# TensorE's expert code as loops over pairs of experts, weight buffers with a period of two experts, and the last output weights in 1 MB pieces

## The chip, the core and the metric

The kernel runs on one core of one Trainium2 chip. Its time is the device time in microseconds (us) of one execution. The engines are TensorE (PE; PEld is its weight load), VectorE (DVE), ScalarE (ACT), GpSimd (POOL) and SyncE (SP). SP issues nearly all transfers; they run on the core's 16 DMA engines.

## The reference: what is computed

One layer on 256 tokens of 1024 float32 values: a norm and an input projection, a state-space branch and an attention branch that are gated and merged, an output projection, cross-attention to a memory of 256 tokens, and then a mixture of 32 experts, which is the part that the change touches:

```
logits = xf @ w_router + b_router ; the best 4 experts of each token, gates = softmax of their logits
for every expert e, with its tokens xb:
    hgl = xb @ w1[e] + b1[e]                        # 1024 -> 2048 (w1: 8.39 MB for one expert)
    glu = min(hgl[:, :1024], 7) ; lin = clip(hgl[:, 1024:], -7, 7)
    act = glu * sigmoid(1.702 * glu) * (lin + 1)
    y   = act @ w2[e] + b2[e]                       # 1024 -> 1024 (w2: 4.19 MB)
out[token] += gate * y ; then a last norm
```

Every weight of the 32 experts is read once from device memory: 32 x 12.58 MB = 402.7 MB.

## The kernel before

**Ahead of the experts** (until about 456 us) come the projections and attentions. Their tiles lie in one arena in SBUF of 25 pages of 1 MB (`PAGE` is 2048 float32 for each of 128 partitions). As pages come free, SP loads the first expert weights into them: 11 halves of 2 MB, each in two pieces of 1 MB (`piece`, L379).

**An expert on TensorE** is `item(i, parts)` (L1014 to L1024). An expert has 64 slots of tokens. In order: `weights_in` (64 matmuls at L965 against w1, in four halves of 2 MB), `scattered` (8 at L933: adds the result of the expert before to the tokens), `gather` (8 at L918: the tokens of the next expert), then transposes (L984 gates, L990 activations, L925 gathered tokens) and two bias matmuls (L941), and `weights_out` (32 at L1010 against w2, in two halves of 2 MB). ACT and DVE do the work between: clips and products (DVE L1780 to L1786), sigmoid (ACT L1340), copies out of PSUM (ACT L1324, L1344, L1348, and L1352 for the result `ys`). TensorE's program is written out: `expert(i)` is called for i = 0 to 29, with the matmuls of the output bias (L1066) between 15 and 16. ACT and DVE run their side of the experts in hardware loops.

**The last two experts** (`last_two`, L1026) are interleaved: input part of 30, its middle, input part of 31, output part of 30, activations of 31, scatter and gates, output part of 31. All of it goes through bank 3 of PSUM.

**The weight buffers.** The stream of weights is cut into chunks `n` of 4 MB, three for an expert: two of w1 and one of w2. `e_at(n)` gives the order, the order of use: (30, w1), (31, w1), (30, w2), (31, w2) at the end. For the first 22 halves, 11 buffers of 2 MB rotate. After that, five buffers of 4 MB rotate (`2 * ((n + 4) % 5) + h`), so chunk n goes where chunk n-5 was. From chunk 21 (expert 7) on, a chunk is one transfer of 4 MB (`whole`, L357); the last chunk of all goes in four pieces of 1 MB with semaphores of their own (L452).

**What orders the transfers.** SP runs one program: for each chunk in the order of the stream it waits until the chunk that lay in the buffer has been used (`e_free`: counters that TensorE raises at the end of each part), and then issues the next transfer. A wait of SP holds back all transfers behind it. All of them go into one queue (q1).

Of the kernel before, what the change touches and what calls it, by code (L numbers as in the profile page):

```python
# [17 lines left out]
D = 1024  # L18
# [14 lines left out]
CHUNKS = 3  # L33
BY_HALF = 21
LAST = CHUNKS * NE - 1
# [10 lines left out]
def layer_program(nc, x, mem, norm_mix_g, w_in, conv_w, conv_b, dt_bias, a_log, d_skip, ssd_norm_g,  # L46
# [52 lines left out]
    with ExitStack() as ctx:  # L99
# [84 lines left out]
        W_AT = (0, 2, 4, 6, 8, 10, 14, 16, 18, 20, 23)  # L184
        prow3 = late[0:2, 1536:2048]
# [114 lines left out]
        last_loaded = [sem(f"last_loaded{k}") for k in range(4)]  # L300
# [13 lines left out]
        def e_at(n):  # L314

            last = CHUNKS * (NE - 2)
            if n < last:
                return n // CHUNKS, n % CHUNKS
            return ((NE - 2, 0), (NE - 2, 1), (NE - 1, 0), (NE - 1, 1), (NE - 2, 2), (NE - 1, 2))[n - last]

        def e_source(n, h):

            i, s = e_at(n)
            if s < 2:
                return w_ein[0, i, 512 * s:512 * (s + 1), :].rearrange("(p h c) n -> p h (c n)", h=2, c=2)[:, h, :]
            return w_eout[0, i].rearrange("(p h c) n -> p h (c n)", h=2, c=4)[:, h, :]

        def e_slot(n, h):

            m = 2 * n + h  # L330
            return m % 11 if m < 22 else 2 * ((n + 4) % 5) + h

        def e_half(n, h):

            return page(W_AT[e_slot(n, h)], 2 * PAGE)

        def e_free(n, h):

            i, s = e_at(n)
            if s == 0:  # L340
                return e_used, 4 * i + h + 1
            if h:
                return (h_psum, y_psum)[s - 1], i + 1
            return e_used, 4 * i + 2 + s

        def by_half(n):
            return n < BY_HALF or n == LAST

        filled, loads = [0] * 11, {}
        for n_ in range(CHUNKS * NE):  # L350
            for h_ in range(2):
                b_ = e_slot(n_, h_) - (0 if by_half(n_) else h_)
                if h_ == 0 or by_half(n_):
                    filled[b_] += 32 if 2 * n_ + h_ < 11 else 16
                loads[n_, h_] = (e_loaded[b_], filled[b_])

        def whole(engine, expert, s, quad):  # L357

            to = page(W_AT[2 * quad], 4 * PAGE)
# [4 lines left out]
            engine.dma_start(to, source).then_inc(e_loaded[2 * quad], 16)  # L364
# [5 lines left out]
        def _(sp_):  # L370
# [8 lines left out]
            def piece(m, k):  # L379

                n, h, cols = m // 2, m % 2, slice(PAGE * k, PAGE * (k + 1))
                sp_.dma_start(e_half(n, h)[:, cols], e_source(n, h)[:, cols]).then_inc(e_loaded[e_slot(n, h)], 16)
# [21 lines left out]
            ahead = [(0, 0), (0, 1), (1, 0), (1, 1), (2, 0), (2, 1), (10, 0), (10, 1)]  # L404
            for u in range(unit("out", 3), unit("cv", 1)):
                load(u)
                if ahead:
                    if ahead[0] == (10, 0):
# [4 lines left out]
            piece(4, 0)  # L413
            load(unit("cv", 2))
            piece(4, 1)
# [4 lines left out]
            piece(3, 0)  # L420
            load(unit("co", 3))
            piece(3, 1)
            for h in range(2):
                piece(8, h)
            sp_.wait_ge(w_lo_ready, 2 * NU)
            for h in range(2):
                piece(6, h)
            sp_.wait_ge(w_done, 2 * NU)
            for m in (5, 7):
                for h in range(2):  # L430
                    piece(m, h)
            sp_.wait_ge(ms_psum, 2)
            for h in range(2):
                piece(9, h)
            sp_.dma_start(gfin, norm_final_g.partition_broadcast(P)).then_inc(ld_g, 16)

            owner = {e_slot(m // 2, m % 2): m for m in range(11)}
            for n in range(CHUNKS, CHUNKS * NE):
                for h in range(2):
                    m = 2 * n + h  # L440
                    if m < 11:
                        continue
                    b = e_slot(n, h)
                    was, owner[b] = owner[b], m
                    if by_half(n) or h:
                        sp_.wait_ge(*e_free(was // 2, was % 2))
                    if n < BY_HALF:
                        sp_.dma_start(e_half(n, h), e_source(n, h)).then_inc(e_loaded[b], 16)
                    elif n == LAST:
                        for k in range(2):  # L450
                            cols = slice(PAGE * k, PAGE * (k + 1))
                            sp_.dma_start(e_half(n, h)[:, cols], e_source(n, h)[:, cols]).then_inc(last_loaded[2 * h + k], 16)  # L452
                    elif h:
                        whole(sp_, *e_at(n), b // 2)
                if n == 5 * CHUNKS:
                    sp_.wait_ge(item_psum, 1)
                    sp_.dma_start(b2[0:NE, :], b_eout[0]).then_inc(ld_b2, 16)
# [4 lines left out]
            with sp_.If(n_items > NE):  # L462
                with sp_.Fori(NE, n_items) as i:
                    e = sp_.value_load(meta[0:1, bass.ds(i, 1)], min_val=0, max_val=NE - 1)
                    sp_.wait_ge(y_psum, i)
                    for s in range(CHUNKS):
                        whole(sp_, e, s, s)
# [80 lines left out]
        def _(pe):  # L548
# [450 lines left out]
            def weights_out(i, parts):  # L999
                pe.wait_ge(at_ready, i + 1)  # L1000
                for h in range(2):
                    w, loaded = parts[4 + h]
                    if loaded:
                        pe.wait_ge(*loaded)
                    for c in range(4):
                        if type(i) is int and i == NE - 1 and c % 2 == 0:
                            pe.wait_ge(last_loaded[2 * h + c // 2], 16)
                        for half in range(2):
                            at = D * c + 512 * half
                            last = mm(ps[64 * half:64 * (half + 1), 3, :], at_cols[:, c, h, :], w[:, at:at + 512],  # L1010
                                      start=(h + c == 0), stop=(h + c == 4))
                    last.then_inc((e_used, y_psum)[h], 1)

# [31 lines left out]
            place = {e_at(n): n for n in range(CHUNKS * NE)}  # L1045

            def parts_of(i):

                out = []
                for s in range(CHUNKS):  # L1050
                    n = place[i, s]
                    for h in range(2):
# [15 lines left out]
            for i in range(NE // 2, NE - 2):  # L1068
                expert(i)
            last_two(NE - 2)  # L1070
            with pe.If(n_items > NE):
                gather(NE + 1)
                gathered_transposes(NE + 1)
                next_bias(NE - 1)
                with pe.Fori(NE, n_items) as i:
                    item(i, [(page(W_AT[2 * s + h], 2 * PAGE), None if h else (e_loaded[2 * s], 16 * i + (filled[2 * s] - 16 * (NE - 1))))
                             for s in range(CHUNKS) for h in range(2)])
# [5 lines left out]
        def _(act):  # L1083
# [262 lines left out]
            def acts(i):  # L1346
                act.wait_ge(at_psum, i + 1)
                A(actT, ps[:, 0, :], ACT.Copy).then_inc(at_ready, 1)  # L1348

            def result(i):  # L1350
                act.wait_ge(y_psum, i + 1)
                A(ys, ps[:, 3, :], ACT.Copy).then_inc(y_ready, 1)  # L1352
# [480 lines left out]
```

## Time and profile before

| | |
|---|---|
| three runs | 1371.81, 1371.67, 1368.5 us; median 1371.67 |
| the profiled execution | 1372.18 us; span in the trace 1370.4 us, mean TensorE clock 0.984 |
| PE busy | 1313.5 us (96% of the span) |
| DVE, ACT, POOL busy | 425.8, 363.0, 34.0 us |
| DMA | 471.86 MB, 344 GB/s over the span |

"Busy" is the union of an engine's instructions. A matmul at L965 shows 592 ns, but they overlap: 64 of them take 13.9 us. Clock 1.00 is 2.4 GHz and 0.5 is 1.2 GHz. The span starts at the first instruction; every time below is in us from there.

### The profile page before, as it was taken

The numbers are of one execution on the slowest core, as the hardware profiler recorded it, in microseconds if no ns is written. First come the engines' busy times: TensorE is split into PE (matmuls) and PEld (weight loads), VectorE is DVE, ScalarE is ACT, GpSimd is POOL, SyncE is SP. The second block draws the span as 40 slices with busy tenths as digits, with TensorE's granted clock in tenths as the row PEclk, the third lists the DMA queues.
The fourth block names the chain that finished last, engine by engine and source line by source line (L and its number), as shares of the span: only waits on it lengthen the run. The fifth ranks groups of instructions, "written<-read, shape, count | busy, mean of one in ns | idle before, by whom it ended". The sixth has DMA issues, their size and how long they took to land.

```text
span 1370.4 us, 17367 instructions
## 1 busy us (share of the span) xinstructions
PE 1313.5 (96%) x7436; PEld 733.1 (53%) x7436; DVE 425.8 (31%) x808; ACT 363.0 (26%) x559; POOL 34.0 (2%) x57
## 2 busy tenths in 40 slices
PE   6999999999999999999999999999899999899997
PEld 6999999999999433333333333333333333333332
DVE  6775657576653311211121112111112111112111
ACT  4854446645443211111111111111111111111102
POOL 2001200001001000000000000000000000000000
PEclk8999999999999999999999999999999999999999
DMA  7545453478856999999999999999999999999994
GB/s 222 157 140 152 141 153 101 130 209 304 302 185 253 407 405 427 418 428 435 428 434 433 429 431 432 432 428 431 430 436 430 429 428 434 435 430 428 430 428 188
DMA packets 87180, 471.86 MB, mean 344 GB/s; under 512 B 7194, under 2 KB 68770, under 8 KB 70212
## 3 DMA queue, kind: packets, MB, share of 16 engines
q1 hardware_dynamic: 86880, 470.71, 85.2%
q8 instruction: 60, 0.98, 0.3%
q10 hardware_dynamic: 228, 0.07, 0.0%
q14 instruction: 12, 0.10, 0.0%
HBM read 469.72 MB, written 1.05 MB: 344 GB/s over the span
## 4 chain that ended last, share of the span: by engine, by line
PE 72%; DMA 25%; ACT 1%; DVE 1%; issue 0%; ACTq 0%; DVEq 0%
DMA arena<-in_w_expert_in 22%; PE ps L965 19%; PE ps L1010 12%; PE ps L617 8%; PE ps L618 7%; PE ps L619 7%; PE ps L933 3%; PE ps L918 3%; DMA arena<-in_w_expert_out 3%; PE ps L608 1%; PE ps L610 1%; PE ps L609 1%; PE ps L925 1%; PE ps L941 1%; PE ps L990 1%; PE ps L984 1%
## 5 line engine op out<-in xcount | busy, mean ns | idle before, releaser
L965 PE MATMUL ps<-arena 128*64 128x512 f32 x2048 | 460.6, 605 | 31.8 <-DMA arena<-in_w_expert_in 31.2
L965 PEld LDWEIGHTS ps<-arena 128*64 128x64 f32 x2048 | 148.3, 139 | 337.2 <-issue 289.0
L1780 DVE TENSOR_SCALAR arena<-ps 128x512 f32<-128x512 f32 x32 | 22.1, 691 | 670.3 <-PE ps L965 670.3
L1010 PE MATMUL ps<-arena 128*64 128x512 f32 x1024 | 226.8, 595 | 3.1 <-DMA arena<-in_w_expert_out 2.6
L617 PE MATMUL ps<-A_hi,w_hi 128*128 128x256 f32 x576 | 168.2, 292 | 5.9 <-DVE A_lo L1404 4.6
L618 PE MATMUL ps<-A_lo,w_hi 128*128 128x256 f32 x576 | 165.1, 287 | 0.0
L619 PE MATMUL ps<-A_hi,w_lo 128*128 128x256 f32 x576 | 165.0, 286 | 0.0
L1437 DVE TENSOR_TENSOR w_lo<-w_raw,w_hi 128x1024 fp32r<-128x1024 f32 x120 | 142.7, 1230 | 60.8 <-ACT w_hi L1116 60.5
L1010 PEld LDWEIGHTS ps<-arena 128*64 128x64 f32 x1024 | 71.1, 137 | 138.9 <-issue 138.2
L1340 ACT ACTIVATE arena<-arena 128x512 f32<-128x512 f32 x32 | 20.1, 629 | 446.4 <-DVE arena L1780 446.4
L1116 ACT ACTIVATE w_hi<-w_raw 128x1024 fp32r<-128x1024 f32 x120 | 120.1, 1048 | 25.7 <-DMA w_raw<-in_w_out 6.7
L617 PEld LDWEIGHTS ps<-A_hi,w_hi 128*128 128x128 f32 x576 | 112.7, 196 | 8.3 <-issue 7.0
L618 PEld LDWEIGHTS ps<-A_lo,w_hi 128*128 128x128 f32 x576 | 112.9, 196 | 0.1
L619 PEld LDWEIGHTS ps<-A_hi,w_lo 128*128 128x128 f32 x576 | 112.7, 196 | 0.0
L1352 ACT ACTIVATE arena<-ps 128x512 f32<-128x512 f32 x32 | 19.1, 597 | 243.9 <-PE ps L1010 243.9
L933 PE MATMUL ps<-arena 64*128 64x512 f32 x264 | 65.6, 615 | 0.7 <-ACT arena L1352 0.7
L918 PE MATMUL ps<-arena,wrt 128*64 128x512 f32 x256 | 62.0, 605 | 0.0
L933 PEld LDWEIGHTS ps<-arena 64*128 64x128 f32 x264 | 22.7, 186 | 42.5 <-issue 40.7
L1727 DVE TENSOR_TENSOR arena<-ps,prm 128x512 f32<-128x512 f32 x32 | 22.1, 691 | 73.8 <-PE ps L925 73.8
L1324 ACT ACTIVATE arena<-ps 128x512 f32<-128x512 f32 x32 | 19.1, 597 | 77.5 <-PE ps L918 77.5
L1340 ACT ACT_TABLE_LOAD x30 | 38.5, 1283 | 1.0 <-issue 0.5
L918 PEld LDWEIGHTS ps<-arena,wrt 128*64 128x64 f32 x256 | 15.6, 136 | 42.1 <-issue 42.1
(300 smaller groups left out, 1337.5 us busy)
## 6 DMA issues: line engine op xcount, KB each, us to landing
arena<-in_w_expert_in SPq DMA_DIRECT2D x50, 4096.0 KB, 38.3
arena<-in_w_expert_out SPq DMA_DIRECT2D x24, 4096.0 KB, 39.8
arena<-in_w_expert_in SPq DMA_DIRECT2D x20, 2048.0 KB, 15.2
w_raw<-in_w_in SPq DMA_DIRECT2D x32, 1024.0 KB, 5.5
arena<-in_w_expert_out SPq DMA_DIRECT2D x11, 2048.0 KB, 15.8
arena<-in_w_expert_in SPq DMA_DIRECT2D x16, 1024.0 KB, 9.8
arena<-in_w_expert_out SPq DMA_DIRECT2D x10, 1024.0 KB, 10.8
w_raw<-in_w_cross_kv SPq DMA_DIRECT2D x8, 1024.0 KB, 8.0
```

The source lines that it names most:

```text
L617: mm(o, w_hi[:, s, k, :], a_hi[:, k, :], start=(k == 0), stop=False)
L618: mm(o, w_hi[:, s, k, :], a_lo[:, k, :], start=False, stop=False)
L619: last = mm(o, w_lo[:, s, k, :], a_hi[:, k, :], start=False, stop=(k == KT - 1))
L918: last = mm(ps[64 * half:64 * (half + 1), 2, :], sel[:, 64 * tb:64 * (tb + 1)], xtok[:, tb, 512 * half:512 * (half + 1)], start=(tb == 0), ...
L933: last = mm(ps[:, 4 + 2 * tb + half, :], sgT[rows, tb * P:(tb + 1) * P], ys[rows, :], start=False, stop=bool(each), skip_group_check=True)
L965: last = mm(ps[64 * half:64 * (half + 1), b, :], xg_cols[:, 2 * h + c, s, :], columns[:, :, half, :], start=False, stop=(s + h + c == 3), ...
L1010: last = mm(ps[64 * half:64 * (half + 1), 3, :], at_cols[:, c, h, :], w[:, at:at + 512], start=(h + c == 0), stop=(h + c == 4))
L1116: A(w_hi[:, p % 4, :, :], raw_w[u % 2][:, :, j * P:(j + 1) * P], ACT.Copy).then_inc(w_hi_ready, 1)
L1340: A(sig, glu, ACT.Sigmoid, scale=ALPHA).then_inc(sig_ready, 1)
L1437: V_.tensor_tensor(w_lo[:, p % 4, :, :], raw_w[u % 2][:, :, j * P:(j + 1) * P], w_hi[:, p % 4, :, :].bitcast(f32), ALU.subtract).then_inc( ...
L1727: V_.tensor_tensor(xgT.rearrange("p (m a j) -> p m a j", m=4, a=2), ps[:, 2, :].rearrange("p (m a j) -> p m a j", m=4, a=2), prm[:, 136:14 ...
L1780: V_.tensor_scalar(glu, ps[:, 0, :], LIMIT, None, ALU.min).then_inc(glu_ready, 1)
```

## The change

Four things change together.

1. TensorE's program for experts 6 to 29 is two hardware loops over pairs of experts (`pairs(3, 5)` and `pairs(5, 15)`), two experts written out in the body. Semaphore targets are computed from the loop's register. Experts 0 to 5 are written out as before, and the output-bias matmuls lie between 9 and 10.
2. Buffers: w1 of an even expert lies in slots 0 to 3, of an odd one in 4 to 7, so w1 of expert i goes where w1 of i-2 was. w2 of experts 0 to 5 rotates over three halves (slots 8, 9, 10), and from expert 6 on it always lies in slots 8 and 9, one buffer of 4 MB. w2 of expert 31 goes to slots 0 and 1, where w1 of 30 was. SP issues transfers in the order in which the buffers come free: at expert i, first w1 of i+2, then w2 of i+1.
3. Whole transfers of 4 MB are used for experts 10 to 29 (before: 7 to 31 but for the last chunk).
4. w2 of experts 30 and 31 comes in eight pieces of 1 MB, each with its semaphore, and TensorE takes each by itself. The output part of 31 goes to bank 2 of PSUM and its activations to `xgT`, so its first piece stands ahead of the scatter of expert 30.

```diff
-CHUNKS = 3
-BY_HALF = 21
-LAST = CHUNKS * NE - 1
+BY_HALF = 10
+BY_THREE = 6
+LAST_TWO = NE - 2
...
-        last_loaded = [sem(f"last_loaded{k}") for k in range(4)]
+        last_loaded = [[sem(f"last_loaded{b}_{k}") for k in range(4)] for b in range(2)]
...
+        def e_slot(i, j):
+
+            if j < 4:
+                return 4 * (i % 2) + j
+            if i == NE - 1:
+                return j - 4
+            return 8 + ((2 * i + j - 4) % 3 if i < BY_THREE else j - 4)
...
+        def e_free(i, j):
+
+            if j in (3, 5):
+                return (h_psum if j == 3 else y_psum), i + 1
+            return e_used, 4 * i + min(j, 3) + 1
+
+        def whole(i, j):
+            return BY_HALF <= i < LAST_TWO
+
+        def in_pieces(i, j):
+            return i >= LAST_TWO and j >= 4
+
+        order = [(i_, j_) for i_ in range(LAST_TWO) for j_ in range(6)]
+        for js in (range(4), range(4, 6)):
+            order += [(i_, j_) for i_ in (LAST_TWO, NE - 1) for j_ in js]
+        follower, filled, loads, owner = {}, [0] * len(W_AT), {}, {}
+        for at in order:
+            b_ = e_slot(*at)
+            if b_ in owner:
+                follower[owner[b_]] = at
...
+            for was in order:
+                if was not in follower:
+                    continue
+                i, j = follower[was]
+                if j % 2 or not whole(i, j):
+                    sp_.wait_ge(*e_free(*was))
+                if in_pieces(i, j):
+                    for k in range(2):
+                        cols = slice(PAGE * k, PAGE * (k + 1))
+                        sp_.dma_start(e_half(i, j)[:, cols],
+                                      e_source(i, j)[:, cols]).then_inc(last_loaded[i - LAST_TWO][2 * (j - 4) + k], 16)
+                elif not whole(i, j):
+                    sp_.dma_start(e_half(i, j), e_source(i, j)).then_inc(e_loaded[e_slot(i, j)], 16)
+                elif j % 2:
+                    load_whole(sp_, i, j // 2, e_slot(i, j - 1))
...
+            def out_pass(cols, bank, w, h, c):
+
+                for half in range(2):
+                    at = D * c + 512 * half
+                    last = mm(ps[64 * half:64 * (half + 1), bank, :], cols[:, c, h, :], w[:, at:at + 512],
+                              start=(h + c == 0), stop=(h + c == 4))
+                return last
...
             def last_two(i):
 
-                first, second = parts_of(i), parts_of(i + 1)
-                weights_in(i, first)
+                def out_piece(b, cols, bank, k):
+
+                    pe.wait_ge(last_loaded[b][k], 16)
+                    for c in (2 * (k % 2), 2 * (k % 2) + 1):
+                        last = out_pass(cols, bank, e_half(i + b, 4 + k // 2), k // 2, c)
+                    return last
+
+                weights_in(i, parts_of(i))
                 scattered(i)
                 gather(i + 2)
                 gates(i)
                 acts(i)
                 gathered_transposes(i + 2)
                 next_bias(i)
-                weights_in(i + 1, second)
+                weights_in(i + 1, parts_of(i + 1))
                 pe.wait_ge(sgt_ready, i + 2)
-                weights_out(i, first)
+                pe.wait_ge(at_ready, i + 1)
+                for k in range(2):
+                    out_piece(0, at_cols, 3, k)
                 acts(i + 1)
+                out_piece(0, at_cols, 3, 2)
+                out_piece(0, at_cols, 3, 3).then_inc(y_psum, 1)
+                pe.wait_ge(at_ready, i + 2)
+                out_piece(1, xg_cols, 2, 0)
                 scattered(i + 1)
                 gates(i + 1)
+                for k in range(1, 4):
+                    last = out_piece(1, xg_cols, 2, k)
+                last.then_inc(y_psum, 1)
                 pe.wait_ge(sgt_ready, i + 3)
-                weights_out(i + 1, second)
...
+            def pair_parts(pair, first, i):
 
                 out = []
-                for s in range(CHUNKS):
-                    n = place[i, s]
-                    for h in range(2):
-                        own = n != LAST and (h == 0 or by_half(n))
-                        out.append((e_half(n, h), loads[n, h] if own else None))
+                for j in range(6):
+                    loaded = loads.get((i, j))
+                    if loaded:
+                        step = 32 if j >= 4 else 16
+                        loaded = loaded[0], step * pair + (loaded[1] - step * first)
+                    out.append((e_half(i, j), loaded))
                 return out
 
-            def expert(i):
+            def pairs(first, end):
+
+                with pe.Fori(first, end) as pair:
+                    for n in range(2):
+                        item(2 * pair + n, pair_parts(pair, first, 2 * first + n))
+
+            for i in range(BY_THREE):
                 item(i, parts_of(i))
-
-            for i in range(NE // 2):
-                expert(i)
+            pairs(BY_THREE // 2, BY_HALF // 2)
...
-            for i in range(NE // 2, NE - 2):
-                expert(i)
-            last_two(NE - 2)
+            pairs(BY_HALF // 2, LAST_TWO // 2)
+            last_two(LAST_TWO)
...
             sigmoid(NE - 1)
+            acts(NE - 1, xgT)
             result(NE - 2)
-            acts(NE - 1)
             gates(NE - 1)
-            result(NE - 1)
+            result(NE - 1, 2)
```

## Rows read from the trace of the kernel before

**Rows 1.** Windows of about one expert: busy us, clock, DMA share, GB/s.
```profile
core 0: us, PE busy (x) PEld busy (x) DVE busy (x) ACT busy (x) POOL busy (x), PEclk, DMA share, GB/s
460.00:489.20 29.20, 29.20 (x146) 11.18 (x142) 5.33 (x14) 6.29 (x12) 0.00 (x0) 1.00 0.94 373
489.20:518.40 29.20, 29.20 (x138) 10.43 (x136) 4.40 (x10) 3.94 (x6) 0.00 (x0) 1.00 1.01 430
576.80:606.00 29.20, 29.20 (x138) 10.25 (x134) 4.40 (x10) 3.94 (x6) 0.00 (x0) 1.00 1.01 430
1190.00:1219.20 29.20, 26.66 (x126) 9.67 (x124) 4.39 (x10) 3.95 (x6) 0.00 (x0) 1.00 1.00 430
```

**Rows 2.** TensorE in order of time (start, us, line): output of 16, expert 17.
```profile
920.56 7.09 PE L1010 MATMUL ps<-arena 128*64 128x512 f32 x32
927.48 13.90 PE L965 MATMUL ps<-arena 128*64 128x512 f32 x64
941.32 1.99 PE L933 MATMUL ps<-arena 64*128 64x512 f32 x8
947.13 7.09 PE L1010 MATMUL ps<-arena 128*64 128x512 f32 x32
```

**Rows 3.** The same view, stalls and clock at experts 15 and 19.
```profile
874.04 8.78 PE L965 MATMUL ps<-arena 128*64 128x512 f32 x32 [2.55 <-DMA arena<-in_w_expert_in]
991.83 7.09 PE L965 MATMUL ps<-arena 128*64 128x512 f32 x32 [2.46 <-DMA arena<-in_w_expert_in]
```

**Rows 4.** The same view, the tail: experts 29, 30 and 31.
```profile
1284.75 8.64 PE L965 MATMUL ps<-arena 128*64 128x512 f32 x32 [2.36 <-DMA arena<-in_w_expert_in]
1299.14 7.09 PE L1010 MATMUL ps<-arena 128*64 128x512 f32 x32
1306.06 7.04 PE L965 MATMUL ps<-arena 128*64 128x512 f32 x32
1313.90 7.09 PE L965 MATMUL ps<-arena 128*64 128x512 f32 x32 [0.81 <-DMA arena<-in_w_expert_in]
1320.92 1.99 PE L933 MATMUL ps<-arena 64*128 64x512 f32 x8
1327.01 13.95 PE L965 MATMUL ps<-arena 128*64 128x512 f32 x64 [0.20 <-DVE arena L1727]
1343.56 7.09 PE L1010 MATMUL ps<-arena 128*64 128x512 f32 x32 [2.60 <-DMA arena<-in_w_expert_out]
1350.58 0.75 PE L990 MATMUL ps<-ident,arena 128*128 128x128 f32 x4
1351.33 1.99 PE L933 MATMUL ps<-arena 64*128 64x512 f32 x8
1353.25 0.44 PE L984 MATMUL ps<-ident,arena 128*128 128x128 f32 x2
1354.16 7.09 PE L1010 MATMUL ps<-arena 128*64 128x512 f32 x32 [0.47 <-ACT arena L1344]
```

**Rows 5.** VectorE in order of time, activations of expert 31.
```profile
1341.01 0.69 DVE L1780 TENSOR_SCALAR arena<-ps 128x512 f32<-128x512 f32 x1 [13.22 <-PE ps L965]
1343.06 0.69 DVE L1786 TENSOR_TENSOR arena<-arena 128x512 f32<-128x512 f32 x1
```

**Rows 6.** Issues of SP in order of time.
```profile
1262.73 31.03 SPq L364 DMA_DIRECT2D arena<-in_w_expert_in  x4
1306.27 0.33 SPq L364 DMA_DIRECT2D arena<-in_w_expert_out  x1
1309.70 4.24 SPq L452 DMA_DIRECT2D arena<-in_w_expert_out  x4
```

**Rows 7.** The four pieces of the last chunk (L452), from issue to landing.
```profile
DMA to landing us min/median/max: 36.2/38.0/39.7
```

**Rows 8.** The page: busy time and instructions; the queue of instruction pages.
```profile
PE 1313.5 (96%) x7436; PEld 733.1 (53%) x7436; DVE 425.8 (31%) x808; ACT 363.0 (26%) x559; POOL 34.0 (2%) x57
q8 instruction: 60, 0.98, 0.3%
```

**Rows 9.** One window from expert 15's stall to expert 29's, columns as in rows 1.
```profile
874.04:1284.75 410.71, 388.65 (x1745) 136.61 (x1745) 61.55 (x140) 55.27 (x84) 0.00 (x0) 0.97 1.00 431
```

**Rows 10.** First loads: issues of SP; transfers at L448; the page's row of gfin.
```profile
444.24 4.20 SPq L382 DMA_DIRECT2D arena<-in_w_expert_in  x4
448.48 0.44 SPq L435 DMA_DIRECT2D gfin<-in_norm_final_g  x1
460.49 0.33 SPq L448 DMA_DIRECT2D arena<-in_w_expert_out  x1
...
482.68 0.33 SPq L448 DMA_DIRECT2D arena<-in_w_expert_in  x1
...
DMA to landing us min/median/max: 7.2/15.8/20.6
...
gfin<-in_norm_final_g SPq DMA_DIRECT2D x1, 512.0 KB, 13.5
```

**Rows 11.** TensorE in order of time, first output part and the next.
```profile
478.99 7.09 PE L1010 MATMUL ps<-arena 128*64 128x512 f32 x32
505.55 7.09 PE L1010 MATMUL ps<-arena 128*64 128x512 f32 x32
```

More of the change, by code:

```diff
@@ L184, in layer_program @@
         W_AT = (0, 2, 4, 6, 8, 10, 14, 16, 18, 20, 23)
+        EXTRA_AT = (0, 2, 8)
         prow3 = late[0:2, 1536:2048]
@@ L328, in e_slot @@
[L328 to L359, printed above, removed]
+        def e_slot(i, j):
[4 more added lines that the diff above has]
+            return 8 + ((2 * i + j - 4) % 3 if i < BY_THREE else j - 4)
@@ new lines, in e_half, with e_source @@
+        def e_half(i, j):
+            return page(W_AT[e_slot(i, j)], 2 * PAGE)
+        def e_source(i, j):
+            if j < 4:
+                rows = slice(512 * (j // 2), 512 * (j // 2 + 1))
+                return w_ein[0, i, rows, :].rearrange("(p h c) n -> p h (c n)", h=2, c=2)[:, j % 2, :]
+            return w_eout[0, i].rearrange("(p h c) n -> p h (c n)", h=2, c=4)[:, j - 4, :]
+        def e_free(i, j):
+            if j in (3, 5):
+                return (h_psum if j == 3 else y_psum), i + 1
+            return e_used, 4 * i + min(j, 3) + 1
@@ new lines, in whole @@
+        def whole(i, j):
[10 more added lines that the diff above has]
+                follower[owner[b_]] = at
+            if not in_pieces(*at) and not (whole(*at) and at[1] % 2):
+                filled[b_] += 16 if b_ in owner else 32
+                loads[at] = (e_loaded[b_], filled[b_])
+            owner[b_] = at
@@ L360, in whole, with load_whole @@
+        def load_whole(engine, expert, s, slot):
             if s < 2:
@@ L363, in whole @@
                 source = w_eout[0, expert].rearrange("(p c) n -> p (c n)", c=8)
-            engine.dma_start(to, source).then_inc(e_loaded[2 * quad], 16)
+            engine.dma_start(page(W_AT[slot], 4 * PAGE), source).then_inc(e_loaded[slot], 16)
         block = ctx.enter_context(nc.Block())
@@ L403, in _ @@
             sp_.wait_ge(b1_ready, 2)
-            ahead = [(0, 0), (0, 1), (1, 0), (1, 1), (2, 0), (2, 1), (10, 0), (10, 1)]
+            ahead = [(i, j, k) for i, j in ((0, 0), (0, 1), (0, 2), (1, 4)) for k in range(2)]
             for u in range(unit("out", 3), unit("cv", 1)):
@@ L407, in _ @@
                 if ahead:
-                    if ahead[0] == (10, 0):
+                    if ahead[0] == (1, 4, 0):
                         sp_.wait_ge(a_lo_ready, SPLIT["u2"] + 4)
@@ L412, in _ @@
             sp_.wait_ge(w_done, 2 * unit("cq", 3) + 2)
-            piece(4, 0)
+            piece(1, 0, 0)
             load(unit("cv", 2))
-            piece(4, 1)
+            piece(1, 0, 1)
             for u in range(unit("cv", 3), unit("co", 2)):
@@ L419, in _ @@
             load(unit("co", 2))
-            piece(3, 0)
+            piece(0, 3, 0)
             load(unit("co", 3))
-            piece(3, 1)
-            for h in range(2):
-                piece(8, h)
+            piece(0, 3, 1)
+            for k in range(2):
+                piece(0, 4, k)
             sp_.wait_ge(w_lo_ready, 2 * NU)
-            for h in range(2):
-                piece(6, h)
+            for k in range(2):
+                piece(1, 2, k)
             sp_.wait_ge(w_done, 2 * NU)
-            for m in (5, 7):
-                for h in range(2):
-                    piece(m, h)
+            for j in (1, 3):
+                for k in range(2):
+                    piece(1, j, k)
@@ L432, in _ @@
             sp_.wait_ge(ms_psum, 2)
-            for h in range(2):
-                piece(9, h)
+            for k in range(2):
+                piece(0, 5, k)
             sp_.dma_start(gfin, norm_final_g.partition_broadcast(P)).then_inc(ld_g, 16)
[L437 to L455, printed above, removed]
@@ new lines, in _ @@
+            for was in order:
[5 more added lines that the diff above has]
+                if in_pieces(i, j):
+                    for k in range(2):
+                        cols = slice(PAGE * k, PAGE * (k + 1))
+                        sp_.dma_start(e_half(i, j)[:, cols],
[4 more added lines that the diff above has]
+                    load_whole(sp_, i, j // 2, e_slot(i, j - 1))
+                if was == (4, 0):
@@ L465, in _ @@
                     sp_.wait_ge(y_psum, i)
-                    for s in range(CHUNKS):
-                        whole(sp_, e, s, s)
+                    for s in range(3):
+                        load_whole(sp_, e, s, EXTRA_AT[s])
             for tb in range(TB):
@@ L1005, in weights_out @@
                     for c in range(4):
[L1006 to L1011, printed above, removed]
-                    last.then_inc((e_used, y_psum)[h], 1)
+                        last = out_pass(at_cols, 3, w, h, c)
+                    last.then_inc((e_used, y_psum)[h], 1)
+            def out_pass(cols, bank, w, h, c):
[4 more added lines that the diff above has]
+                return last
             def item(i, parts):
@@ L1075, in _ @@
                 with pe.Fori(NE, n_items) as i:
-                    item(i, [(page(W_AT[2 * s + h], 2 * PAGE), None if h else (e_loaded[2 * s], 16 * i + (filled[2 * s] - 16 * (NE - 1))))
-                             for s in range(CHUNKS) for h in range(2)])
+                    item(i, [(page(W_AT[EXTRA_AT[s]] + 2 * h, 2 * PAGE),
+                              None if h else (e_loaded[EXTRA_AT[s]], 16 * i + (filled[EXTRA_AT[s]] - 16 * (NE - 1))))
+                             for s in range(3) for h in range(2)])
             pe.wait_ge(y_ready, n_items + 1)
@@ L1344, in gates, with acts, result @@
                 A(sgT, ps[:, 3, 0:S], ACT.Copy).then_inc(sgt_ready, 1)
-            def acts(i):
+            def acts(i, to=actT):
                 act.wait_ge(at_psum, i + 1)
-                A(actT, ps[:, 0, :], ACT.Copy).then_inc(at_ready, 1)
-            def result(i):
+                A(to, ps[:, 0, :], ACT.Copy).then_inc(at_ready, 1)
+            def result(i, bank=3):
                 act.wait_ge(y_psum, i + 1)
-                A(ys, ps[:, 3, :], ACT.Copy).then_inc(y_ready, 1)
+                A(ys, ps[:, bank, :], ACT.Copy).then_inc(y_ready, 1)
             def item(i):
```

21 lines of the change are left out of this document (5 added, 16 removed).

## The prediction

> **What bounds the kernel now.** I read the windows of one expert's length first. In the expert part the DMA engines move 430 GB/s at a busy share of 1.00 from the second window on, while TensorE's busy time falls from 29.20 of 29.20 us to 26.66 [rows 1]. So from some point the weights set the pace. Then TensorE in order of time. Without a stall one expert takes 947.13 - 920.56 = 26.57 us [rows 2]. With stalls, 14 experts (second w1 chunk of 15 to that of 29, 874.04 to 1284.75) take 410.71 us, 29.34 each [rows 3, 4], so a chunk of 4 MB takes 9.78 us. TensorE is 2.77 us an expert faster than its weights, and every expert waits once, for the second chunk of w1.
>
> The tail decides what the change is worth, so I read it instruction by instruction [rows 4]. The second w1 chunk of expert 30 is there at 1313.90. Four chunks follow it in the stream: 1313.9 + 4 x 9.78 = 1353.0 for the end of all loads. The last pieces say the same: issued from 1309.70 on, the last about 1313.6 [rows 6], landing within 39.7 us [rows 7], 1353.3. TensorE's last expert matmul ends at 1354.16 + 7.09 = 1361.25. So the tail behind the last byte is 8 us: TensorE reaches the output part of 30 at about 1341 (1327.01 + 13.95), waits until 1343.56 for its chunk as one whole, and has then 7.02 (output of 30), 0.75, 1.92, about 0.9 and 7.09 us of work in a row. After 1361.25 the same 9 us of scatter, norm and stores follow in both kernels.
>
> Three things are to be priced: when the loads end, what TensorE still has to do behind the load that holds it, and what the loops cost.
>
> **The order of the loads: this is the largest term.** Before, chunks arrive in the order in which they are used. After, SP issues w1 of i+2 when w1 of i has been read, and w2 of i+1 only when w2 of i has been read, which is behind it. Both go into one queue, and the last five issues, some 38 us from landing with four chunks ahead of them [rows 6, 7], say that this queue is served in order. So the stream at the end is w1(30), w2(29), w1(31), w2(30), w2(31), where it was w2(29), w1(30), w1(31), w2(30), w2(31). The chunk in front of the last four is now w2 of expert 29. It lands when w1 of 30 did, T = 1313.9, and only then can TensorE start the output part of 29. It has all of 30 and 31 still before it, on weights that are by then in place:
> - output of 29: 1306.06 - 1299.14 = 6.92 [rows 4]
> - input of 30: 941.32 - 927.48 = 13.84 [rows 2]
> - middle of 30: 1327.01 - 1320.92 = 6.09 [rows 4]
> - input of 31: 13.84, which makes 1354.59
> - output of 30, 7.02 (1350.58 - 1343.56), transposes 0.75, output of 31, 7.02, scatter 1.92 (1353.25 - 1351.33), gates 0.44 [rows 4]: 17.15
>
> This ends at 1371.74, against 1361.25: **+10.5 us**. Work in the tail has no load to wait for any more: the last byte is there at about 1353, before the input of 31 is done. Hence the pieces of 1 MB and their semaphores gain nothing by arriving early. What part 4 of the change does save is the 0.5 us wait of the last output part for ACT (0.47 in rows 4), and it is already in the sum. Its activations hide too: the chain on DVE takes 2.74 us from the end of the input (1341.01 to 1343.06 + 0.69, [rows 5]), and the two first pieces, 3.5 us, lie over it.
>
> Does TensorE wait long enough to arrive at T at all? Unstalled it would be at the output of 29 at 478.99 + 29 x 26.57 + 4 (bias) = 1253.5 [rows 2, 11], 60 us before T. Yes.
>
> **Do the DMA engines stay full with one buffer for w2?** When w2 of i has landed (t), the engines have w1 of i+2 ahead of them, 19.6 us. w2 of i+1 is issued at t + 6.9, 12.7 us before its turn. w1 of i+3 is issued from t + 6.9 + 13.8 on, its turn is at t + 29.3. So they stay full, and the stall only moves, from the second chunk of w1 to w2. Cost 0. If this cover went, each microsecond of a gap in every expert would cost 24 us.
>
> **First loads.** The same pages are filled in the same order; what changes is which weights lie in them. The second half of w2 of expert 0 becomes the last (issued by 448.4; the transfer behind it lands within 13.5 us, at 462, [rows 10]) and is needed at 478.99 + 3.5 [rows 11]. The second half of w2 of expert 1 is issued at 482.68 instead of 460.5, lands 7.2 to 20.6 us later, by 503.6 [rows 10], and is needed at 509.0 (505.55 + 3.5, [rows 11]). Cost 0, at most the 1 or 2 us by which such a stall would delay a release while the engines are full anyway. Three more experts by halves: the windows of halves and of whole chunks both show 430 [rows 1]. Cost 0, bounds 0 and +1.
>
> **The loops, on the DMA side.** TensorE's code comes in pages: 60 packets for 0.98 MB, 0.3% of 16 engines' span [rows 8], so 0.003 x 1370 x 16 / 60 = 1.1 us of one DMA engine each. 7436 matmuls and as many weight loads [rows 8] are 14872 instructions, 248 a page, and an expert has 2 x 124, so one page an expert. The loops of ACT and DVE leave no pages in that count. A page delays one engine of 16, and a chunk is there only when the last engine is done. Over the 410.71 us the engines moved 431 GB/s [rows 9], 177.0 MB, while 14 experts need 14 x 12.58 = 176.2: 0.8 MB or 2.0 us (1.5 to 2.5 by the rounding) that the leading engines are ahead and that help nobody. That is 0.14 us a page, and 1.1/16 = 0.07 for its own time: 0.21 us. Of the 24 pages of experts 6 to 29 about 19 go (two bodies of two experts need 2 to 3 each): 19 x 0.21 = **-4.0 us** at T. Bounds: 0 (the loops fetch again at each turn), and -19 x 0.25 = -5 by the upper rounding.
>
> **The loops, on TensorE.** The trace has no loop on TensorE. About 14 waits of an expert now need a computed target, and each pair has a branch. Lower bound 0, since waits for other engines are under way meanwhile, as on DVE and ACT. The slack above it is 29.34 - 0.21 - 26.57 = 2.6 us an expert, 5.1 a pair; below that it costs nothing, since T is set by the loads. I take 0. Above it each further microsecond an expert costs 24 us.
>
> The page Runtime: NRT & Kernel Launch of the Trainium skill (section Instruction fetch mechanics) speaks against the loops: a taken branch to a target outside the window that is held makes the engine wait for the page's DMA. Advanced Engine Details and Errata (section ISA Cache) gives TensorE 128 KB, at its 256 instructions for 16 KB some 2048 as an estimate, and by that a body of two experts, some 530, stays. No row here shows TensorE branching. By the first the -4 would go, by the second it stays.
>
> **Clock.** After some stalls of about 2.5 us, 32 matmuls take 8.78 instead of 7.09 us (874.04), after others not (991.83) [rows 3]. While the loads set the pace that is free. In the tail before there was none after 1299. Now 58 us of TensorE work follow a stall at T with no slack: half of 1.7, **+0.8 us** (0 to 1.7).
>
> **Sum.** 10.5 - 4.0 + 0.8 = +7.3 us. Span 1370.4 + 7.3 = 1377.7. The profiled execution, 1372.18, is 1.8 above its span and 0.5 above the median of the runs, so against the median: 1371.7 + 7.3 = **1379.0 us**, 0.5% slower. Its own range is 1374 to 1384.
>
> **Rivals.**
> - *The pieces work, faster.* If w2 of 29 landed in time for its use, the loads' end would set the end: piece by piece, TensorE would finish 1.8 us behind the last byte. 1353.2 - 4.0 + 1.8 = 1351.0 instead of 1361.25, that is 1361.5 us. It decides where TensorE is through with the input of 31 before w2 of 30 is there; by my sum it is 11 us late (1354.6 against 1343.5). For it: the tail of 8 us is real [rows 4]. Against it: it needs the queue to be served out of order, and the 38 us to landing [rows 7] say in order. 0.13.
> - *The code is fetched anew at each turn.* Same sum without the -4.0: 1383.0. A wait of one or two pages at each branch, 1.1 to 2.2 us by [rows 8], fits in the 5.1 us of slack. For it: 2 to 3 pages a body is more than a reader ahead of a straight program need keep. Against it: the other engines' loops show no pages, but their bodies are small. 0.17.
> - *The loops become the bound.* Targets and branches cost over 2.6 us an expert. At 4 us: 24 x 1.4 = 34 on top, 1413. Against it: 14 waits would have to cost 0.19 us each with nothing over them, while TensorE in its middle part is always busy. 0.08.
>
> **How the numbers follow.** The forecast has 0.62, of which 0.12 lies within 0.3% (below 1375.8, if the pages are worth more or the middle hides more); 0.3%, 4.1 us, is about what a measurement of this kernel can tell from no change. Faster 0.13, same 0.12, slower 0.50 + 0.17 + 0.08 = 0.75. The range is 1370 to 1389: it takes in the forecast, the second rival with the clock's bound and the mild end of the third; left out are the first and most of the third, 0.2.
>
> **What would show it.** After: TensorE waits about 2.6 us for w2, ahead of each output part, from about 9 on and not at all for w1; the output part of 29 starts at about 1310 and from there to the end no wait for a DMA; the last transfer lands 20 us or more before the last expert matmul ends. q8 falls from 60 to about 40 packets; if it stays at 60 the second rival holds. Expert windows at 26.57 us or more without any DMA wait mean the third. Waits for single pieces of w2 of 30 and 31 mean the first, and that the order of landing is not what I take it for.

## The result, and the profile after

Six runs of the changed kernel: 1382.65, 1381.43, 1383.47, 1377.36, 1376.94 and 1382.36 us, median 1381.89, against 1371.74 for the kernel before (six runs). The ratio is 1.007, 95% interval 1.0056 to 1.0084: 0.7% slower. The forecast was 1379.0 with a range of 1370 to 1389.

| profiled execution | before | after |
|---|---|---|
| time, span (us) | 1372.18, 1370.4 | 1382.65, 1380.9 |
| S: first matmul of the experts | 456.80 | 457.67 |
| T: landing with four chunks to come | 1313.90 (w1 of 30) | 1312.48 (w2 of 29) |
| last expert matmul ends | 1361.25 | 1371.72 |

The first thing to read is TensorE in order of time in the tail. Columns: start, us, line (L963 input part, L1013 output part, L931 scatter).

```profile
1283.19 7.09 PE L1013 MATMUL ps<-arena 128*64 128x512 f32 x32 [0.86 <-DMA arena<-in_w_expert_out]
...
1312.48 8.54 PE L1013 MATMUL ps<-arena 128*64 128x512 f32 x32 [2.66 <-DMA arena<-in_w_expert_out]
1320.85 13.90 PE L963 MATMUL ps<-arena 128*64 128x512 f32 x64
...
1340.77 13.95 PE L963 MATMUL ps<-arena 128*64 128x512 f32 x64 [0.19 <-DVE arena L1751]
1354.55 3.60 PE L1013 MATMUL ps<-arena 128*64 128x512 f32 x16
1358.08 0.75 PE L989 MATMUL ps<-ident,arena 128*128 128x128 f32 x4
1358.76 5.37 PE L1013 MATMUL ps<-arena 128*64 128x512 f32 x24
1364.06 1.99 PE L931 MATMUL ps<-arena 64*128 64x512 f32 x8
...
1366.35 5.37 PE L1013 MATMUL ps<-arena 128*64 128x512 f32 x24
```

The last wait for a load in the program is at 1312.48, for w2 of expert 29. From there TensorE works for 59.24 us without waiting for a byte, where in [rows 4] it met its last load at 1343.56. None of the eight pieces is waited for: the last is issued at 1328.3 and lands within 23.9 us, by 1352.2, and the first is taken at 1354.55. That the input part of 31 ends within 0.04 us of the 1354.59 in the sum is luck: the 1354.59 stands without the terms of the pages and the clock, and with them it would be 1351.4. Here the landing was 1.42 us earlier than its T, and the output part of 29 took 8.54 instead of 7.09 us, 1.45 more (granted clock 0.83 from 1312.48 to 1321.02). The waits, in total (us, times, longest), say the same of the whole run: no wait for w1 is left.

```profile
PEld ps L1013 <- DMA arena<-in_w_expert_out: 48.3, 24, 4.1
...
PE ps L1013 <- DMA arena<-in_w_expert_out: 39.2, 22, 3.8
```

On the loops, the page after, its queues:

```profile
q1 hardware_dynamic: 89184, 470.71, 84.1%
q8 instruction: 40, 0.66, 0.2%
```

20 of 60 instruction packets are gone [rows 8], one for each of the 24 experts in the loops but the four that stand in the two bodies, so the bodies are not fetched again at each turn. What the loop costs TensorE shows in the output parts of experts 5, 6 and 7, where it hardly waits yet:

```profile
612.75 7.09 PE L1013 MATMUL ps<-arena 128*64 128x512 f32 x32
...
639.33 7.09 PE L1013 MATMUL ps<-arena 128*64 128x512 f32 x32
646.25 13.90 PE L963 MATMUL ps<-arena 128*64 128x512 f32 x64
...
665.90 7.32 PE L1013 MATMUL ps<-arena 128*64 128x512 f32 x32
673.05 13.90 PE L963 MATMUL ps<-arena 128*64 128x512 f32 x64
```

From the output part of 6 to that of 7, both in the loop, it is 665.90 - 639.33 = 26.57 us, as written out [rows 2], so the computed targets cost nothing. The output part of 7, the last of the first turn, is longer: 673.05 - 665.90 = 7.15 instead of 6.92 us. That looks like the price of the turn, and it is not. Its weight loads show where the 0.23 us lie:

```profile
668.53 0.14 PEld L1013 LDWEIGHTS ps<-arena 128*64 128x64 f32 x2 [0.29 <-issue]
669.57 0.20 PEld L1013 LDWEIGHTS ps<-arena 128*64 128x64 f32 x4 [0.89 <-DMA arena<-in_w_expert_out]
...
672.20 0.14 PEld L1013 LDWEIGHTS ps<-arena 128*64 128x64 f32 x2 [0.28 <-issue]
672.63 0.14 PEld L963 LDWEIGHTS ps<-arena 128*64 128x64 f32 x2 [0.28 <-issue]
```

The gap is in the middle, a wait for the second half of the weights. The turn lies between the last two lines, and there the next weight load follows after 0.43 us, as everywhere. The same holds at all 23 borders of an output and an input part between 600 and 1300 us that have nothing between them, whether a turn lies there or not: 0.42 or 0.43 us. So a turn of the loop costs TensorE nothing that this trace shows.

Windows after, first in the part with transfers by halves, then in the steady part (columns as in rows 1):

```profile
518.40:664.40 146.00, 146.00 (x683) 52.16 (x680) 24.87 (x55) 20.79 (x32) 0.00 (x0) 1.00 1.01 425
874.00:1282.00 408.00, 385.21 (x1736) 136.01 (x1736) 60.27 (x136) 55.26 (x84) 0.00 (x0) 0.97 1.00 431
```

### The profile page after: what moved, and what is told of

Same layout as the page of the kernel before. It is cut to its first block, busy times and chain, and to the rows that moved or that the text cites. A ratio compares the mean times of both kernels' runs of the same rounds, so it can differ in the third digit from the quotient of the medians.

```text
span 1380.9 us, 17493 instructions
## 1 busy us (share of the span) xinstructions
PE 1318.8 (96%) x7436; PEld 734.1 (53%) x7436; DVE 426.2 (31%) x808; ACT 363.0 (26%) x559; POOL 34.0 (2%) x57
## 3 DMA queue, kind: packets, MB, share of 16 engines
q1 hardware_dynamic: 89184, 470.71, 84.1%
## 4 chain that ended last, share of the span: by engine, by line
PE 64%; DMA 33%; ACT 1%; DVE 1%; issue 0%; ACTq 0%; DVEq 0%
DMA arena<-in_w_expert_out 32%; PE ps L1013 17%; PE ps L963 12%; PE ps L615 7%; PE ps L616 7%; PE ps L617 7%; PE ps L931 2%; PE ps L916 2%; PE ps L606 1%; PE ps L608 1%; PE ps L607 1%; DMA w_raw<-in_w_fox_branch 1%; PE ps L923 1%; PE ps L819 1%; DVE w_lo L1461 1%; PE ps L798 1%
## 5 line engine op out<-in xcount | busy, mean ns | idle before, releaser
L963 PE MATMUL ps<-arena 128*64 128x512 f32 x2048 | 447.0, 594 | 0.5 <-DVE arena L1751 0.5
L963 PEld LDWEIGHTS ps<-arena 128*64 128x64 f32 x2048 | 146.0, 137 | 294.1 <-issue 292.7
L1013 PE MATMUL ps<-arena 128*64 128x512 f32 x1024 | 244.4, 631 | 39.2 <-DMA arena<-in_w_expert_out 39.2
L1013 PEld LDWEIGHTS ps<-arena 128*64 128x64 f32 x1024 | 74.1, 145 | 190.2 <-issue 141.7
L931 PE MATMUL ps<-arena 64*128 64x512 f32 x264 | 65.6, 615 | 0.7 <-ACT arena L1376 0.7
L931 PEld LDWEIGHTS ps<-arena 64*128 64x128 f32 x264 | 22.7, 186 | 43.1 <-issue 41.5
```

Source lines behind the costliest of these rows:

```text
L931: last = mm(ps[:, 4 + 2 * tb + half, :], sgT[rows, tb * P:(tb + 1) * P], ys[rows, :], start=False, stop=bool(each), skip_group_check=True)
L963: last = mm(ps[64 * half:64 * (half + 1), b, :], xg_cols[:, 2 * h + c, s, :], columns[:, :, half, :], start=False, stop=(s + h + c == 3), ...
L1013: last = mm(ps[64 * half:64 * (half + 1), bank, :], cols[:, c, h, :], w[:, at:at + 512], start=(h + c == 0), stop=(h + c == 4))
```

## The experiments

The kernel before, measured beside them, had a median of 1372.0 for e1 to e4 and of 1371.9 for e5 to e8. Beside the medians I use the profile of one execution of each: S is not the same in each execution (452.97 to 457.67), so landings and ends are counted from S. They are in the table that follows the experiments.

**e1, the order alone.** The kernel before, with w2 of 29 behind w1 of 30 in the stream:

```diff
-            last = CHUNKS * (NE - 2)
+            last = CHUNKS * (NE - 3) + 2
-            return ((NE - 2, 0), (NE - 2, 1), (NE - 1, 0), (NE - 1, 1), (NE - 2, 2), (NE - 1, 2))[n - last]
+            return ((NE - 2, 0), (NE - 2, 1), (NE - 3, 2), (NE - 1, 0), (NE - 1, 1), (NE - 2, 2), (NE - 1, 2))[n - last]
```

> The kernel before with one change: w2 of expert 29 stands behind w1 of expert 30 in the order of the loads. Theory (the order sets the tail): the output part of 29 starts when the fourth chunk from the end is still to come, about 1313, and 58 to 60 us of TensorE work follow with no wait for a load; the last expert matmul ends at 1313.9 + 40.7 + 7.0 + 0.75 + 1.9 + 0.9 + 7.1 = 1372 instead of 1361, so +11 us against the kernel before (+10 to +13 with the clock). Rival (the queue or the buffers are not what holds the tail; the loops are what made the change slower): within 3 us of the kernel before.

Measured: 1384.19 (4 runs), ratio 1.0094 (1.008 to 1.0109), +12.2 us. Its trace:

```profile
1282.57 7.09 PE L965 MATMUL ps<-arena 128*64 128x512 f32 x32 [2.37 <-DMA arena<-in_w_expert_in]
...
1311.80 9.32 PE L1010 MATMUL ps<-arena 128*64 128x512 f32 x32 [16.32 <-DMA arena<-in_w_expert_out]
1320.94 13.91 PE L965 MATMUL ps<-arena 128*64 128x512 f32 x64
...
1365.22 7.09 PE L1010 MATMUL ps<-arena 128*64 128x512 f32 x32 [0.47 <-ACT arena L1344]
```

No loop, the old ring of five buffers, no pieces, and one chunk set back behind two others at the very end of 96: TensorE stands still for 16.32 us at the output of 29, and from S on the end comes 13.5 us later than before (table below). The tail is longer by 60.51 - 47.35 = 13.16 us. Of this 2.23 are the lower clock (9.32 instead of 7.09 us, granted clock 0.76), and the 10.9 that are left are close to the 10.5 of the prediction plus the 0.47 us wait for ACT, which stays here. This shows the order of landing as the cause of the loss: alone it costs at least all that the change lost.

**e2, experts 6 to 29 written out.** The changed kernel without its loops:

```diff
-                with pe.Fori(first, end) as pair:
-                    for n in range(2):
-                        item(2 * pair + n, pair_parts(pair, first, 2 * first + n))
+                for i in range(2 * first, 2 * end):
+                    item(i, parts_of(i))
```

> The changed kernel with experts 6 to 29 written out, everything else as changed. Theory (the loops only take instruction pages away, and give back about 0.2 us a page): 60 instruction packets again instead of 40, an expert takes 29.34 us instead of 29.15, the output part of 29 starts 3 to 4 us later, and the time is 3 to 4 us above the changed kernel, some 14 us above the one before. Rival (the loops cost TensorE time, in branches or targets): faster than the changed kernel, by up to the 10 us.

Measured: 1382.74 (5 runs, 1379.88 to 1385.64), ratio 1.0087 (1.0074 to 1.01). 60 packets again. The landing came 858.17 us after S against 854.81 and 854.91 in two profiles of the changed kernel: 3.3 us later, as expected. The median does not show it: it is only 0.9 us above that of e5, where I had expected 3 to 4, a difference inside the scatter of these runs. The profiled execution was the shortest of the five, with an S of 452.98. In it the lower clock fell on the output of 28, so that TensorE came to that of 29 later, waited 0.98 us instead of 2.66 and ran it at the full clock, which gave back 1.45:

```profile
1281.83 8.78 PE L1013 MATMUL ps<-arena 128*64 128x512 f32 x32 [2.51 <-DMA arena<-in_w_expert_out]
...
1311.15 7.09 PE L1013 MATMUL ps<-arena 128*64 128x512 f32 x32 [0.98 <-DMA arena<-in_w_expert_out]
```

The rival, loops that cost time, falls: taking them out made nothing faster.

**e3, the pieces alone.** The kernel before, w2 of 30 and 31 in pieces, output of 31 in bank 2 (the code of the change, over the old stream):

```diff
-            return n < BY_HALF or n == LAST
+            return n < BY_HALF or n >= LAST - 1
...
-                weights_out(i, first)
+                pe.wait_ge(at_ready, i + 1)
+                for k in range(2):
+                    out_piece(0, at_cols, 3, k)
                 acts(i + 1)
+                out_piece(0, at_cols, 3, 2)
+                out_piece(0, at_cols, 3, 3).then_inc(y_psum, 1)
+                pe.wait_ge(at_ready, i + 2)
+                out_piece(1, xg_cols, 2, 0)
                 scattered(i + 1)
                 gates(i + 1)
...
```

> The kernel before with the fourth part of the change alone: w2 of experts 30 and 31 in pieces of 1 MB, output of 31 in bank 2 of PSUM. The order of the loads is the one of use. Theory: TensorE waits for the loads here, so the pieces count: the last expert matmul ends about 1.8 to 2 us behind the last byte (1353.3), at 1355.2 instead of 1361.25: -6 us. Rival (the tail is held by the chain over ACT and the scatter, not by the load): -0.5 us, the wait of the last output part for ACT, and no more.

Measured: 1370.53 (12 runs), ratio 0.9987 (0.9978 to 0.9996): -1.5 us, a miss by 4.5. The trace says why:

```profile
1313.66 8.78 PE L965 MATMUL ps<-arena 128*64 128x512 f32 x32 [2.37 <-DMA arena<-in_w_expert_in]
...
1328.45 13.95 PE L965 MATMUL ps<-arena 128*64 128x512 f32 x64 [0.19 <-DVE arena L1745]
1342.24 3.60 PE L1013 MATMUL ps<-arena 128*64 128x512 f32 x16
...
1346.45 5.37 PE L1013 MATMUL ps<-arena 128*64 128x512 f32 x24
...
1354.04 5.37 PE L1013 MATMUL ps<-arena 128*64 128x512 f32 x24
```

I had counted from the last byte. But TensorE has 1359.41 - 1342.24 = 17.17 us of its own behind the input part of 31, and comes from w1 of 30 without a further wait: 1313.66 + 8.71 + 6.08 + 13.79 + 17.17 = 1359.41. No piece was waited for. So in the old order two bounds lie close together, the loads' end and TensorE behind the second w1 chunk of 30, and the pieces only take the first away. Here 1.7 us of the lower clock fell on that path too (8.78 instead of 7.09 us, granted clock 0.80), so at the full clock the pieces are worth about 3.3 us in this tail and not 1.6; e8 shows it.

**e4, a loop over five experts.** Experts 10 to 29 of the kernel before in 4 turns of five, the period of its five buffers; the stream is untouched, and the matmuls of the output bias move from behind expert 15 to behind 9:

```diff
-            for i in range(NE // 2):
+            for i in range(10):
...
-            for i in range(NE // 2, NE - 2):
-                expert(i)
+            with pe.Fori(2, (NE - 2) // 5) as turn:
+                for n in range(5):
+                    item(5 * turn + n, [(w, (loaded[0], 48 * turn + (loaded[1] - 96)) if loaded else None)
+                                        for w, loaded in parts_of(10 + n)])
```

> The kernel before with TensorE's experts 10 to 29 in one hardware loop over five experts, the period of its ring of five buffers, so the order of the loads is untouched. Theory (pages cost 0.2 us each): 14 to 15 pages fewer, -3 us. Rivals: the body of five experts (some 1300 instructions, over 5 pages) is fetched anew at each of the 4 turns, 60 packets again and no gain, 0; or branches and targets cost time in the tail, +1 or more.

Measured: 1368.6 (7 runs), ratio 0.9972 (0.9961 to 0.9983): -3.4 us. The page of e4:

```profile
q8 instruction: 45, 0.74, 0.2%
```

15 pages fewer, the landing 854.36 after S instead of 857.10: 2.74 us, 0.18 us a page. A body of five experts was not fetched anew either.

**e5, the changed kernel again,** beside the next three.

> The changed kernel once more, beside the others on the same chip. +10 us against the kernel before. The written-out form measured +10.7 us, so if a page costs what I took (0.2 us) this one should be 3 us below that, near +8; if the loops are worth nothing in this order of loads it is +10 to +11. The profile tells by when the output part of 29 starts and whether that part falls into a stretch of the lower clock.

Measured: 1381.81 (5 runs, 1381.27 to 1382.17), ratio 1.0073 (1.006 to 1.0086), +9.9 us. The lower clock fell on the output of 29 once more:

```profile
1311.83 8.59 PE L1013 MATMUL ps<-arena 128*64 128x512 f32 x32 [2.64 <-DMA arena<-in_w_expert_out]
```

**e6, all four pieces waited for at once.**

```diff
-                    pe.wait_ge(last_loaded[b][k], 16)
+                    if k == 0:
+                        for n in range(4):
+                            pe.wait_ge(last_loaded[b][n], 16)
```

> The changed kernel, with TensorE waiting for all four pieces of w2 of an expert (30, 31) before it takes the first. Theory (TensorE is behind the loads in the whole tail, every piece has landed when it comes): the same time as the changed kernel within 1 us. Rival (the pieces do carry part of the tail): slower by up to 5 us.

Measured: 1381.96 (5 runs), ratio 1.0076 (1.0063 to 1.0089); 0.15 us from e5. In the order of the change the pieces carry nothing.

**e7, half of w2 of 29 early.** In the changed kernel slot 10 is free from expert 6 on. The first half goes there, ahead of w1 of 30:

```diff
+            if (i, j) == (NE - 3, 4):
+                return 10
...
+                if was == (27, 5):
+                    sp_.dma_start(e_half(29, 4), e_source(29, 4)).then_inc(e_loaded[10], 16)
```

> The changed kernel with the first half (2 MB) of w2 of expert 29 in the free slot 10, loaded before w1 of 30; experts 28 and 29 written out. The second half still lands where it did. Theory (end = landing of what holds the tail + TensorE's work behind it): 16 matmuls, 3.5 us, move ahead of the landing, so 3.5 us less than the changed kernel. Rival (something else in the tail): no difference.

Measured: 1377.77 (5 runs), ratio 1.0042 (1.0029 to 1.0055): 4.0 us less than e5, 3.5 expected. The output of 29 now starts before its second half is there (issued at 1288.90, landed 22.4 us later at 1311.3) and does not wait for it, since it comes to it at 1311.8:

```profile
1308.36 7.09 PE L1019 MATMUL ps<-arena 128*64 128x512 f32 x32
```

That the two numbers lie so close is partly luck. From S on the end comes 914.19 - 909.99 = 4.2 us earlier than in e5. Of this 2.7 are the earlier start of the output of 29 (852.21 after S instead of 854.91); the other 1.5 are the lower clock, which fell on it in e5 and not here. The 3.5 us of work did move ahead, but the second half landed 0.2 us later than in e5 and 0.5 us before TensorE came to it.

**e8, what helped, together.** e3 and e4 in one kernel:

> Two parts that helped alone, together: the loop of five experts over the kernel before (-3.4 us measured) and w2 of 30 and 31 in pieces with bank 2 (-1.5 us measured). If they add, -5 us against the kernel before, 1367. The pieces alone gave less than I had said since TensorE's own 17.2 us behind the input of 31 became the end, with no wait for a piece; that is a bound that both share: second w1 chunk of 30 at about 1311 + 7.0 + 6.1 + 13.8 + 17.2 = 1355 for the last expert matmul, 1.7 later if the lower clock falls in.

Measured: 1363.79 (6 runs, 1361.96 to 1367.4), ratio 0.9948 (0.9934 to 0.9962): -8.1 us, faster than both kernels. Of this the trace shows 5.8 us from S on (904.45 to 898.62): 2.5 at the landing, 3.3 in the tail, which ran at the full clock. That is the 1.6 of e3 and the 1.7 of lower clock in it:

```profile
1307.54 7.09 PE L965 MATMUL ps<-arena 128*64 128x512 f32 x32 [0.65 <-DMA arena<-in_w_expert_in]
...
1320.64 13.95 PE L965 MATMUL ps<-arena 128*64 128x512 f32 x64 [0.20 <-DVE arena L1747]
1334.42 3.60 PE L1013 MATMUL ps<-arena 128*64 128x512 f32 x16
...
1346.22 5.37 PE L1013 MATMUL ps<-arena 128*64 128x512 f32 x24
```

The rest of the 9.6 us between the two profiled executions is an early S (452.97 instead of 456.80). As e1, e2 and e6 had an S as early or nearly so, I take it for a chance of the execution and 5.8 us for what the kernel gains; the median of six runs, three near 1362 and three from 1365 to 1367, may hold some of that chance too.

All profiles, in us: S, the landing with four chunks to come after S, TensorE from there to the end of its last expert matmul, and that end after S:

| | S | landing - S | tail | end - S |
|---|---|---|---|---|
| before | 456.80 | 857.10 | 47.35 | 904.45 |
| after | 457.67 | 854.81 | 59.24 | 914.05 |
| e1 order alone | 454.37 | 857.43 | 60.51 | 917.94 |
| e2 written out | 452.98 | 858.17 | 57.80 | 915.97 |
| e3 pieces alone | 456.54 | 857.12 | 45.75 | 902.87 |
| e4 loop of five | 456.77 | 854.36 | 46.93 | 901.29 |
| e5 after again | 456.92 | 854.91 | 59.28 | 914.19 |
| e6 waited at once | 454.15 | 854.85 | 59.48 | 914.33 |
| e7 half early | 456.15 | no wait there | | 909.99 |
| e8 e3 and e4 | 452.97 | 854.57 | 44.05 | 898.62 |

## Why the prediction was right

- **The order of the loads, +10.5.** Right, in mechanism and size. The tail without the low clock is 59.24 - 1.45 = 57.79 us against 47.35: +10.4. e1 shows it alone, 10.9 with the wait for ACT, and e7 shows that the end moves with the start of the output of 29.
- **The pieces gain nothing.** Right (e6). My rival gave them 10 us with the pages if the order were harmless. In a harmless order they are worth little too, 1.5 us (e3) and 3.3 at the full clock (e8), since I left TensorE's own 17.2 us out of that case.
- **DMA engines stay full.** Right: share 1.00 in the steady window, and TensorE waits at most once an expert from 10 on, only for w2.
- **Transfers and buffers, 0 (0 to +1).** Too small. e2 has the pages of the kernel before and lands 1.07 us later after S (0.74 to 1.07 against before, e1 and e3). The window from 518 to 664 moved 425 GB/s in the changed kernel, where the one before has 428 there:

```profile
518.40:664.40 146.00, 146.00 (x685) 52.84 (x681) 24.86 (x55) 21.72 (x34) 0.00 (x0) 1.00 1.01 428
```

  The packets went from 86880 to 89184 in the whole run. Which part of the change does it, more halves or their slots, was not tried apart.
- **Pages, -4.0.** The mis-sized term. Right is that 20 pages went, where I had said 19, and that the landing moved with them. The price is 3.3 / 20 = 0.17 us (e2 against after and e5) and 2.74 / 15 = 0.18 us (e4 against before), not 0.21: -3.4 instead of -4.0. That a page costs more than its own time because the other engines run ahead was argued from rows and is shown by no run. With the +1.1 above the landing moved by -2.3.
- **Loops on TensorE, 0.** Right: 26.57 us an expert, and no cost of a turn that the weight loads show. By the page Runtime: NRT & Kernel Launch of the Trainium skill (section Instruction fetch mechanics) a branch beyond the held window would fetch; by the page Advanced Engine Details and Errata of the Trainium skill (section ISA Cache) TensorE has 128 KB, which would hold the body. The traces agree with the 128 KB: 40 and 45 packets. The same section also says "Only 2 cache lines!", of 16 KB; that does not fit e4, whose body of five pages was not fetched anew.
- **Clock, +0.8 (0 to 1.7).** The size was a choice between two values. It was +1.45 in the profiled execution, 1.50 in e5, 1.69 in e6 and, outside my bound, 2.23 in e1. These four had waited 2.64 us or more for the output of 29; e2 had waited 0.98 us and ran it at the full clock. The wait alone does not decide it: in e6 the output of 28 followed a wait of 2.50 us and took 7.09. Two of the six runs of the change lie at 1377 instead of 1382. The clock in the tail can't explain 5 us; an early S can explain most, since it moves by up to 4.7 us between executions, and the one of e6 that was profiled (1379.42, 2.5 us under its median) has its S 2.8 us earlier than e5 and the same end after S. For the two runs themselves it stays open.

The sum, from S on: 10.4 - 2.3 + 1.45 = +9.6 in place of +7.3, and S itself was 0.9 later in that execution: +10.5 in the spans, +10.1 in the medians.

## What to carry to other kernels

Where loads set the pace and a queue serves them in order, the end is the landing of the load that holds the tail plus all work behind it, so look at which load that is before counting the last byte. A buffer plan in which something needed earlier is loaded later cost next to nothing in the steady state here (its stall only moved) and 10.4 us at the end, where no later work could take it up. Choose the loop's period from the buffers' (five experts here) and not the buffers from the loop's.

## What the runs showed that I had not expected

- Code costs more than its bytes: 15 pages of 16 KB less took 0.18 us each off the landing, where the 1.1 us that I had estimated for each on one of 16 engines would be 0.07. Why it is more is open.
- TensorE went from the end of a loop's body to its start without a gap, with bodies of two experts. A body of five experts (620 matmuls and as many weight loads) ran 4 turns with 45 pages in all.
- The first matmul of the experts started between 452.97 and 457.67 us in ten profiles. It is not the kernel: the changed one started at 457.67 and 456.92, and at 454.15 in e6, which differs from it only in the last two experts. Comparing spans of single profiles would have shown 4 us of it as an effect. It goes with the granted clock (the column behind POOL's) between 200 and 300 us, which is 1.00 in the four profiles with an S up to 454.4 and 0.99 in the six from 456.1 on; here the kernel before and e8:

```profile
200.00:300.00 100.00, 98.84 (x771) 95.50 (x771) 64.81 (x123) 55.92 (x98) 0.00 (x0) 0.99 0.50 148
```

```profile
200.00:300.00 100.00, 98.84 (x781) 95.50 (x780) 67.09 (x126) 57.79 (x101) 0.00 (x0) 1.00 0.50 156
```

  The clock of the first 100 us does not go with it: it is 0.95 in the kernel before, and 1.00 in e3, whose S (456.54) is as late. What sets off the lower clock there, no run tells.
